# Norm seams of a two-block transformer kernel: order of high and low parts, VectorE's norms and GpSimd's weight pieces

## The chip, the core and the metric

The kernel runs on one core of a Trainium2 chip. The metric is the device time of one execution in microseconds. The engines are TensorE (PE; its weight loads are PEld), VectorE (DVE), ScalarE (ACT), GpSimd (POOL) and SyncE (SP), which issues the weight loads. Each has its own instruction stream, and they meet at semaphores.

## The reference, cut to what matters

Everything is float32: 512 tokens, width 1024. Two blocks of two layers follow each other. The running sum h has a normed copy taken of it before every large product, and the product is added to it:

```
y = h * rsqrt(mean(h*h, axis=-1) + EPS) * gain      # rms norm over the 1024 features
h = h + dsa_attention(norm(h)); h = h + relu(norm(h) @ w_up)**2 @ w_down           # first block, layer 0
k, v, decay = norm(h) @ w_kv; h = h + fox_attention(norm(h), k, v); h = h + mlp(norm(h))
h = norm(h) * g_final
h = h + g1 * gqa_attention(norm(h)*(1+sc1) + sh1); h = h + g2 * mlp(norm(h)*(1+sc2) + sh2)   # second block
h = h + g1 * chunked_gmlp(...); h = h + g2 * mlp(...)
```

In the second block a shift is added behind the norm (sh1, sh2), and the gains, shifts and gates come from a product with ada_w.

## The kernel before, in words

**Data.** h lies transposed in SBUF as HT: eight chunks of 128 features (KC = 8), each 512 tokens wide. The kernel keeps float32 accuracy with three products of numbers of shorter mantissa: an operand x is split in a high part (ScalarE's copy to the type fp32r, in Xhi) and a low part (x less the high part, in Xlo), a weight likewise in whi and wlo. Each product is high times high, high times low and low times high, into one PSUM bank.

**Units of weights.** A GEMM takes its weights in units of 256 columns (1 MB). SyncE loads unit u into raw[u % 2] once the low parts of unit u-2 are out (semaphore lo_done). ScalarE makes whi in two pieces of four chunks (split, L976 to L988, semaphore hi_done), GpSimd makes wlo from them in two pieces (split, L1889 to L1896, lo_done). TensorE waits for each piece ahead of the chunk that needs it (wait_unit_half). A unit has two tiles (j) of 128 output features; each tile is 24 matmuls over the eight chunks, 512 columns wide. The GEMMs "vb" and "gv" have tokens as rows and take a unit as four chunks by 512 columns (tm_wide).

**A seam.** Where a norm stands between two GEMMs and its input is the sum of the first GEMM's outputs, the work is cut in two halves of 256 tokens (h = 0, 1). There are seven, called after the sum (EVENTS): oa, m0, ob, m1, oc, m2 and go, before the normed inputs m0, kv, m1, c, m2, g and m3 (HALVED). m1, oc, m2 and go stand before norms with a shift; m1 has two sums for each chunk, since a final norm and the next block's norm fall together. At a seam:

- TensorE computes the last unit half by half (fm, last). In half 1, after five of the eight chunks of its first tile, come the means of half 0 (norm_means, four matmuls of one column with the mean vector, L450), and after that tile the reciprocal roots are spread to rows by two transposes (norm_rows, L636) into bank 6.
- VectorE (seam, from L1444) adds the last two tiles to HT half by half (add_half, L1407 or L1409), adds their squares to the running sums (add_square_half, L1437), takes reciprocals (recip, L1442), then writes the normed chunk to tmp (L1473, whose second input is the row in PSUM) and the low part Xlo (low, L1460). It takes the norms of chunks one by one and behind each the low part of the chunk two before. A tmp slot of half 0 is used by chunk c and again by chunk c + 4.
- ScalarE (seam, from L1052) squares the last chunks (L1042), takes roots (root, L1048), copies each normed chunk to Xhi (L1068, or L1070 with a shift) and among these makes the two high pieces of the second unit behind the seam.
- GpSimd (seam, from L1911) writes a few of the low parts at the seams oa, m0 and ob (pool_lows: chunks 1 and 3 of half 0 and 3, 5 and 7 of half 1) and, after those of half 0, both low pieces of the second unit. The pieces of the first unit behind the seam were made during the last GEMM's last unit (units).
- TensorE takes the first unit behind the norm half by half (fm with halved, L461 to L492; tm_wide with halved for gv, L583 to L606). For each chunk it waits for the high part and issues four matmuls with it, waits for the low part and issues two with it. Among the chunks of half 0 it puts the means (after chunk 3) and rows (after chunk 5) of half 1. In tm_wide a half has four chunks, and all four banks must be free before it starts; the last one is freed by the last add_half.

For the input g the norms come in the order 0 to 5, 8 to 11, 6, 7, 12 to 15 (fill_order), where 8 to 15 are half 1.

Of the kernel before, what the change touches and what calls it, by code (L numbers as in the profile page):

```python
# [68 lines left out]
SHARED = ("a", "m0", "kv", "qb", "m1")  # L69
# [5 lines left out]
def fill_order(f):  # L75

    if f == "g":
        return [0, 1, 2, 3, 4, 5, 8, 9, 10, 11, 6, 7, 12, 13, 14, 15]
    return list(range(2 * KC if f in HALVED else KC))


def pool_lows(f):

    return () if f not in SHARED else (1, 3, 11, 13, 15) if f in HALVED else (1, 4, 7)

# [50 lines left out]
def body(nc, ctx, t, consts, out):  # L136
# [286 lines left out]
    def tensor_program(pe):  # L423
# [36 lines left out]
        def fm(name, source, chunk, after=None, first=None, halved=None, last=None):  # L460
# [8 lines left out]
            if halved:  # L469
# [3 lines left out]
                for h in range(2):  # L473
                    for c in range(KC):
# [105 lines left out]
        def tm_wide(name, chunk, after=None, halved=None):  # L580
# [5 lines left out]
            if halved:  # L586
# [4 lines left out]
                for h in range(2):  # L591
                    for c in range(KC // 2):
# [3 lines left out]
                        for q in (2 * h, 2 * h + 1):  # L596
                            pe.matmul(bank[(gm.tile + q) % 4][:], Xhi[:, c, q * P:(q + 1) * P], hi[:, c, :], start=(c == 0), stop=False)
                            pe.matmul(bank[(gm.tile + q) % 4][:], Xhi[:, c, q * P:(q + 1) * P], lo[:, c, :], start=False, stop=False)
                        wait_part(halved, KC * h + c)
                        for q in (2 * h, 2 * h + 1):  # L600
                            m = pe.matmul(bank[(gm.tile + q) % 4][:], Xlo[:, c, q * P:(q + 1) * P], hi[:, c, :], start=False, stop=False)
                        if h == 0 and c == 1:
                            norm_means(e, 1, 1)
                        if h == 0 and c == 2:
                            norm_rows(e, 1)
# [362 lines left out]

    def xq_base(f):
# [4 lines left out]
    def scalar_program(act):  # L974
# [77 lines left out]
        def seam(e, name, f, shift, gain=None):  # L1052
# [7 lines left out]
            for p, k in enumerate(fill_order(f)):  # L1060
                h, c = k // KC, k % KC
                act_until.wait_ge(xq_done, xq_base(f) + p + 1)
# [4 lines left out]
                if shift is None:  # L1067
                    act.activation(Xhi[:, c, tokens(h)], tmp[c % 4][:, tokens(h)], ACT_F.Copy).then_inc(x_hi, 1)  # L1068
                else:
                    act.activation(Xhi[:, c, tokens(h)], tmp[c % 4][:, tokens(h)], ACT_F.Identity, bias=shift[:, c:c + 1]).then_inc(x_hi, 1)  # L1070
                if p == 3:
# [279 lines left out]
    def vector_program(dve):  # L1351
# [92 lines left out]
        def seam(e, name, f, gain, shift, gate=None, both=1):  # L1444

            g, n, order = GEMM[name].end - 2, EVENTS.index(e), fill_order(f)
# [6 lines left out]
            def low(k):  # L1453
                if k in pool_lows(f):
                    return
                h, c = k // KC, k % KC
                q, hi, lo = tmp[c % 4][:, tokens(h)], Xhi[:, c, tokens(h)].bitcast(F32), Xlo[:, c, tokens(h)]
                dve_until.wait_ge(x_hi, high_parts(f, k))
                add = 0.0 if shift is None else shift[:, c:c + 1]
                dve.scalar_tensor_tensor(lo, q, add, hi, ALU.add, ALU.subtract).then_inc(x_lo, 1)  # L1460
            for p, k in enumerate(order):
                h, c = k // KC, k % KC
                if h == 0 and c >= KC - 2:
                    dve_until.wait_ge(half_set, 2 * n + c - KC + 3)
                else:
                    dve_until.wait_ge(h_set, h_at[c])
                if c >= 4:
                    by_dve, by_pool = low_parts(f, k - 4)
                    dve_until.wait_ge(x_lo, by_dve)
# [664 lines left out]
```

## Time and profile before

| | us |
|---|---|
| median of 3 runs (lowest, highest) | 2625.74 (2623.57, 2627.0) |
| profiled execution, its own time | 2622.09 |
| its span, first to last instruction | 2620.4 |
| mean granted TensorE clock | 0.998 |
| weights and tables read from HBM | 270.19 MB, 104 GB/s over the span |

The profile is of one execution. The span is the time between its first and last instruction; the execution's own time is 1.7 us longer, and it lies 3.65 us under the median. Times in rows are from the span's start. An engine's busy time counts its instructions' spans, which on TensorE overlap, since matmuls are pipelined: the distance from one start to the next is the better measure there. A bracket behind a row gives the idle time before it and what ended that.

### The profile page before, as it was taken

Reading aid. Unit: us, or ns where it says so; the run is one execution under the profiler, and the core shown is the slowest. Engines: PE = TensorE matmul, PEld = TensorE weight load, DVE = VectorE, ACT = ScalarE, POOL = GpSimd, SP = SyncE. Lnnn points to the kernel's source line nnn. Section 1 sums busy time; section 2 is a strip of 40 time slices with the busy share of each in tenths; the row PEclk is TensorE's granted clock in tenths of the full one; section 3 lists DMA queues with packets and bytes.
Section 4 is the critical chain, followed back from the end, with each engine's and each line's share of the span. In section 5 each row is a group of like instructions: output and inputs, shape, how many; then the busy total and the mean of one; then the engine's idle time right before and its main releaser. Section 6 shows DMA issues by size and latency. Waiting matters only on the chain.

```text
span 2620.4 us, 34369 instructions
## 1 busy us (share of the span) xinstructions
PE 2550.3 (97%) x13922; PEld 2088.1 (80%) x13922; DVE 1341.1 (51%) x2288; ACT 992.9 (38%) x1685; POOL 1248.5 (48%) x624
## 2 busy tenths in 40 slices
PE   8989999999999999999999999999999999999999
PEld 5667888888776888888877888888888888888887
DVE  4873899843036599992786531223435223532121
ACT  4474423223347432232467432232324223432231
POOL 4865444444457454444487444444443444444442
PEclk9999999999999999999999999999999999999999
DMA  4102555532320355542210233323422222233322
GB/s 139 58 32 65 173 194 181 184 115 78 97 81 2 114 192 193 193 161 97 97 65 18 81 97 97 97 97 114 136 81 81 97 97 81 81 97 97 99 98 77
DMA packets 260897, 277.12 MB, mean 106 GB/s; under 512 B 7172, under 2 KB 249476, under 8 KB 260484
## 3 DMA queue, kind: packets, MB, share of 16 engines
q1 hardware_dynamic: 259140, 272.31, 32.1%
q8 instruction: 110, 1.80, 0.3%
q10 hardware_dynamic: 1600, 2.62, 0.3%
q14 instruction: 47, 0.39, 0.0%
HBM read 270.19 MB, written 2.10 MB: 104 GB/s over the span
## 4 chain that ended last, share of the span: by engine, by line
PE 83%; DVE 10%; issue 3%; ACT 3%; POOL 1%; DMA 0%; SPq 0%; ACTq 0%; DVEq 0%
PE bank L529 21%; PE bank L530 21%; PE bank L531 21%; DVE acc L1568 3%; PE bank L622 2%; PE bank L624 2%; PE bank L623 2%; PE bank L708 2%; PE bank L663 2%; DVE tmp L1603 2%; PE bank L691 1%; DVE Hlo L1606 1%; PE bank L484 1%; DVE Xlo L1460 1%; PE bank L936 1%
## 5 line engine op out<-in xcount | busy, mean ns | idle before, releaser
L1896 POOL TENSOR_TENSOR wlo<-raw,whi 128x1024 fp32r<-128x1024 f32 (+1 forms) x408 | 990.2, 2448 | 1213.4 <-ACT whi L988 1213.4
L988 ACT ACTIVATE whi<-raw 128x1024 fp32r<-128x1024 f32 (+1 forms) x408 | 405.6, 1040 | 572.6 <-PE bank L531 495.9
L529 PE MATMUL bank<-Xhi,whi 128*128 128x512 f32 (+1 forms) x1568 | 620.5, 396 | 1.4 <-POOL wlo L1896 1.4
L530 PE MATMUL bank<-Xlo,whi 128*128 128x512 f32 (+1 forms) x1568 | 611.4, 390 | 0.0
L531 PE MATMUL bank<-Xhi,wlo 128*128 128x512 f32 (+1 forms) x1568 | 610.5, 389 | 0.0
L529 PE MATMUL bank<-Hhi,whi 128*128 128x512 f32 x976 | 381.9, 391 | 0.0
L530 PE MATMUL bank<-Hlo,whi 128*128 128x512 f32 x976 | 380.3, 390 | 0.0
L531 PE MATMUL bank<-Hhi,wlo 128*128 128x512 f32 x976 | 379.7, 389 | 0.0
L529 PEld LDWEIGHTS bank<-Xhi,whi 128*128 128x128 f32 (+1 forms) x1568 | 293.3, 187 | 70.1 <-issue 6.6
L531 PEld LDWEIGHTS bank<-Xhi,wlo 128*128 128x128 f32 (+1 forms) x1568 | 293.4, 187 | 63.8
L530 PEld LDWEIGHTS bank<-Xlo,whi 128*128 128x128 f32 (+1 forms) x1568 | 293.4, 187 | 61.4 <-issue 1.7
L1568 DVE SCALAR_TENSOR_TENSOR acc<-ada,cond,acc 128x256 f32<-128x256 f32 x336 | 272.7, 812 | 12.0
L1394 DVE SCALAR_TENSOR_TENSOR HT<-bank,MOD,HT 128x512 f32<-128x512 f32 x90 | 67.3, 751 | 385.3 <-PE bank L531 365.9
L1603 DVE SCALAR_TENSOR_TENSOR tmp<-tmp 128x512 f32<-128x512 f32 x128 | 134.1, 1048 | 229.9 <-ACT tmp L1132 229.9
L1132 ACT ACTIVATE tmp<-bank 128x512 f32<-128x512 f32 x128 | 76.6, 598 | 407.7 <-PE bank L531 400.0
L531 PEld LDWEIGHTS bank<-Hhi,wlo 128*128 128x128 f32 x976 | 183.3, 188 | 38.5
L529 PEld LDWEIGHTS bank<-Hhi,whi 128*128 128x128 f32 x976 | 183.2, 188 | 37.8
L530 PEld LDWEIGHTS bank<-Hlo,whi 128*128 128x128 f32 x976 | 183.3, 188 | 37.5
L1606 DVE SCALAR_TENSOR_TENSOR Hlo<-tmp,Hhi 128x512 fp32r<-128x512 f32 x128 | 116.8, 913 | 13.9 <-ACT Hhi L1136 0.5
L1392 DVE TENSOR_TENSOR HT<-bank,HT 128x512 f32<-128x512 f32 x72 | 49.0, 690 | 142.8 <-PE bank L531 142.8
L622 PE MATMUL bank<-whi,Xhi 128*128 128x512 f32 x240 | 94.6, 394 | 0.0
L623 PE MATMUL bank<-wlo,Xhi 128*128 128x512 f32 x240 | 93.5, 389 | 0.0
(303 smaller groups left out, 3475.5 us busy)
## 6 DMA issues: line engine op xcount, KB each, us to landing
ada<-in_ada_w SPq DMA_DIRECT2D x48, 1024.0 KB, 5.1
raw<-in_w_up SPq DMA_DIRECT2D x32, 1024.0 KB, 5.4
raw<-in_w_down SPq DMA_DIRECT2D x32, 1024.0 KB, 5.0
raw<-in_mlp_w_in SPq DMA_DIRECT2D x32, 1024.0 KB, 5.3
raw<-in_mlp_w_out SPq DMA_DIRECT2D x32, 1024.0 KB, 5.1
raw<-in_gmlp_w_in SPq DMA_DIRECT2D x24, 1024.0 KB, 5.0
raw<-in_gmlp_w_out SPq DMA_DIRECT2D x12, 1024.0 KB, 5.2
raw<-in_w_in_a SPq DMA_DIRECT2D x8, 1024.0 KB, 5.2
```

The lines of the kernel that those rows point to most:

```text
L529: pe.matmul(b[0:rows, :], whi[s][:, c, j:j + rows], hi[:, c, :], start=(c == 0), stop=False)
L530: pe.matmul(b[0:rows, :], whi[s][:, c, j:j + rows], lo[:, c, :], start=False, stop=False)
L531: m = pe.matmul(b[0:rows, :], wlo[s][:, c, j:j + rows], hi[:, c, :], start=False, stop=(c == KC - 1))
L622: pe.matmul(b[:], Xhi[:, c, q * P:(q + 1) * P], hi[:, k, :], start=(c == 0), stop=False)
L623: pe.matmul(b[:], Xhi[:, c, q * P:(q + 1) * P], lo[:, k, :], start=False, stop=False)
L988: act.activation(whi[u % 2][:, c0:c1, 0:k], src[:, c0:c1, 0:k], ACT_F.Copy).then_inc(hi_done, 1)
L1132: act.activation(tmp[v % 2][:], bank[(gm.tile + o) % 4][:], ACT_F.Relu).then_inc(up_q, 1)
L1394: d = dve.scalar_tensor_tensor(HT[:, o, :], b[:], gate[:, o:o + 1], HT[:, o, :], ALU.mult, ALU.add)
L1568: dve.scalar_tensor_tensor(a[:], src[:, c, :], cd[:, c:c + 1], a[:], ALU.mult, ALU.add).then_inc(ada_step, 1)
L1603: dve.scalar_tensor_tensor(r[:], tmp[v % 2][:], 1.0, tmp[v % 2][:], ALU.mult, ALU.mult).then_inc(up_r, 1)
L1606: dve.scalar_tensor_tensor(Hlo[g % 2][:, o, :], r[:], 1.0, Hhi[g % 2][:, o, :].bitcast(F32), ALU.mult, ALU.subtract).then_inc(h_lo, 1)
L1896: pool.tensor_tensor(wlo[u % 2][:, c0:c1, 0:k], src[:, c0:c1, 0:k], whi[u % 2][:, c0:c1, 0:k].bitcast(F32), ALU.subtract).then_inc(lo_done, 1)
```

## The change

Five things are done at the seams.

1. TensorE, first unit behind a norm: for each half all high parts of the chunks are taken first, then all low parts. The means of half 1 stand after chunk 5 (chunk 2 in tm_wide), the rows of half 1 between the high and the low parts of half 0.
2. VectorE: per half eight norms in a row, then eight low parts in a row. The second sum of chunk 6 stands after the fourth norm of half 0, the add of chunk 7 after the eighth, its sum after the second low part, the reciprocal after the sixth. Low parts without a shift are a tensor_tensor instead of a scalar_tensor_tensor with the constant 0. The eight norms have eight slots: chunks 0 to 3 lie in the first halves of the four tmp tiles, 4 to 7 in the second halves.
3. GpSimd makes no low parts of activations at seams any more; VectorE makes all of them.
4. GpSimd's weight pieces get waits. The second piece of the first unit behind the seam waits until both sums of half 0 are done (sum_half). The first piece of the second unit waits for the eighth low part of half 0, its second piece for the last low part of half 1; for g it has no wait of its own.
5. ScalarE: the second unit's first high piece comes after the eight copies of half 0 and ahead of the second root, its second high piece after the last copy of half 1 (after the fourth for g). The order for g is now 0 to 15.

```diff
-SHARED = ("a", "m0", "kv", "qb", "m1")
+SHARED = ("a", "qb")
...
 # TensorE, fm with halved (tm_wide alike, with means after chunk 2)
                             pe.matmul(b[:, tokens(h)], wlo[s][:, c, j * P:(j + 1) * P], hi[:, c, tokens(h)], start=False, stop=False)
+                        if h == 0 and c == 5:
+                            norm_means(e, 1, 1 + (e == "m1"))
+                    if h == 0:
+                        norm_rows(e, 1)
+                    for c in range(KC):
                         wait_part(halved, KC * h + c)
...
-                        if h == 0 and c == 3:
-                            norm_means(e, 1, 1 + (e == "m1"))
-                        if h == 0 and c == 5:
-                            norm_rows(e, 1)
...
 # ScalarE, seam
+            for h in range(2):
...
+                for c in range(KC):
+                    act_until.wait_ge(xq_done, xq_base(f) + KC * h + c + 1)
...
+                    if h and c == (3 if f == "g" else 7):
+                        split(u + 1, (1,))
+                if h == 0:
                     square_half(e, g + 1, KC - 1, 1, gain)
                     split(u + 1, (0,))
-                if p == 5:
                     root(e, 1)
-                if p == 6:
-                    split(u + 1, (1,))
...
 # VectorE, seam (normed(c) is tmp[c % 4][:, tokens(c // 4)])
+            for h in range(2):
+                for c in range(KC):
...
+                    dve.scalar_tensor_tensor(normed(c), HT[:, c, tokens(h)], gain[:, c:c + 1], bank[6 + h][:, tokens(h)], ALU.mult, ALU.mult).then_inc(xq_done, 1)
+                    if h == 0 and c == 3:
+                        add_square_half(e, KC - 2, 1, both)
+                if h == 0:
+                    add_half(e, g + 1, KC - 1, 1, gate)
+                for c in range(KC):
...
+                    if shift is None:
+                        dve.tensor_tensor(lo, normed(c), hi, ALU.subtract).then_inc(x_lo, 1)
+                    else:
+                        dve.scalar_tensor_tensor(lo, normed(c), shift[:, c:c + 1], hi, ALU.add, ALU.subtract).then_inc(x_lo, 1)
+                    if h == 0 and c == 1:
+                        add_square_half(e, KC - 1, 1, both)
+                    if h == 0 and c == 5:
+                        recip(e, 1)
...
 # GpSimd, units (last is the event's name in the last GEMM before a seam)
-                    split(gm.unit + i + 1)
+                    split(gm.unit + i + 1, (0,))
+                    if last and i == len(gm.widths) - 1:
+                        pool_until.wait_ge(sum_half, square_base(last)[2] + 2 * (1 + (last == "m1")))
+                    split(gm.unit + i + 1, (1,))
...
 # GpSimd, seam
+            u = GEMM[name].unit + len(GEMM[name].widths) + 1
+            pool_until.wait_ge(x_lo, low_parts(f, KC - 1)[0])
+            split(u, (0,))
+            if f != "g":
+                pool_until.wait_ge(x_lo, low_parts(f, 2 * KC - 1)[0])
+            split(u, (1,))
```

## Rows read from the trace of the kernel before

**Rows 1.** The page, part 1: busy us (share of the span) and instructions.

```profile
PE 2550.3 (97%) x13922; PEld 2088.1 (80%) x13922; DVE 1341.1 (51%) x2288; ACT 992.9 (38%) x1685; POOL 1248.5 (48%) x624
```

**Rows 2.** Waits of TensorE: who for whom, us in total, times, longest.

```profile
PE bank L484 <- DVE Xlo L1460: 16.6, 15, 1.9
...
PE bank L450 <- DVE rstd L1437: 5.5, 6, 1.3
...
PE bank L450 <- DVE gained L1437: 2.4, 1, 2.4
...
PE bank L601 <- DVE Xlo L1460: 1.1, 2, 0.9
```

**Rows 3.** Timelines of VectorE and TensorE, seam m2: start, us, instruction, idle before.

```profile
1830.09 0.48 DVE L1409 SCALAR_TENSOR_TENSOR HT<-bank,MOD,HT 128x256 f32<-128x256 f32 x1
...
1830.93 0.47 PE L597 MATMUL bank<-whi,Xhi 128*128 128x512 f32 x1 [1.06 <-DVE HT L1409]
```

**Rows 4.** Timeline of TensorE, seam oa.

```profile
257.32 0.28 PE L550 MATMUL bank<-Xhi,wlo 128*128 128x256 f32 x1
258.81 0.60 PE L450 MATMUL bank<-mean,rstd 128*128 128x1 f32 x4 [1.21 <-DVE rstd L1437]
...
263.54 0.28 PE L480 MATMUL bank<-Xhi,whi 128*128 128x256 f32 x1
...
264.25 0.28 PE L480 MATMUL bank<-Xhi,whi 128*128 128x256 f32 x1
...
270.00 0.29 PE L481 MATMUL bank<-Xhi,wlo 128*128 128x256 f32 x1
272.00 0.50 PE L484 MATMUL bank<-Xlo,whi 128*128 128x256 f32 x2 [1.71 <-DVE Xlo L1460]
```

**Rows 5.** Timeline of VectorE, seam oa.

```profile
255.19 2.33 DVE L1437 SCALAR_TENSOR_TENSOR rstd<-rstd,held 128x256 f32<-128x256 f32 x1 [1.74 <-ACT held L1042]
...
260.97 0.47 DVE L1473 SCALAR_TENSOR_TENSOR tmp<-HT,V,bank 128x256 f32<-128x256 f32 x1
...
263.74 0.42 DVE L1407 TENSOR_TENSOR HT<-bank,HT 128x256 f32<-128x256 f32 x1 [0.26 <-PE bank L550]
...
267.34 0.48 DVE L1473 SCALAR_TENSOR_TENSOR tmp<-HT,V,bank 128x256 f32<-128x256 f32 x1
...
270.23 1.71 DVE L1460 SCALAR_TENSOR_TENSOR Xlo<-tmp,Xhi 128x256 fp32r<-128x256 f32 x1
```

**Rows 6.** Timeline of GpSimd, seam oa.

```profile
252.47 4.77 POOL L1896 TENSOR_TENSOR wlo<-raw,whi 128x1024 fp32r<-128x1024 f32 x2 [6.12 <-ACT whi L988]
...
265.64 2.37 POOL L1896 TENSOR_TENSOR wlo<-raw,whi 128x1024 fp32r<-128x1024 f32 x1 [0.89 <-ACT whi L988]
269.30 2.36 POOL L1896 TENSOR_TENSOR wlo<-raw,whi 128x1024 fp32r<-128x1024 f32 x1 [1.29 <-ACT whi L988]
```

**Rows 7.** Windows at m1: stretch, length, busy by engine, granted clock, DMA share, GB/s.

```profile
1252.00:1254.00 2.00, 1.96 (x14) 1.96 (x15) 0.17 (x1) 0.41 (x2) 0.00 (x0) 0.85 0.00 0
1254.00:1256.00 2.00, 2.00 (x11) 2.00 (x11) 1.04 (x3) 0.66 (x2) 0.00 (x0) 0.50 0.00 0
1256.00:1258.00 2.00, 2.00 (x16) 2.00 (x16) 2.00 (x6) 1.47 (x4) 0.00 (x0) 0.80 0.00 0
```

**Rows 8.** Timelines of VectorE and TensorE, seam m1.

```profile
1247.73 2.61 DVE L1437 SCALAR_TENSOR_TENSOR gained<-gained,held 128x256 f32<-128x256 f32 x1
...
1252.04 0.61 PE L450 MATMUL bank<-mean,rstd 128*128 128x1 f32 x4 [2.41 <-DVE gained L1437]
```

**Rows 9.** Timelines of VectorE and ScalarE: norms (oa), low parts (oc), a high piece.

```profile
261.88 0.87 DVE L1473 SCALAR_TENSOR_TENSOR tmp<-HT,V,bank 128x256 f32<-128x256 f32 x2
...
1488.32 1.26 DVE L1460 SCALAR_TENSOR_TENSOR Xlo<-tmp,MOD,Xhi 128x256 fp32r<-128x256 f32 x3
...
264.52 1.05 ACT L988 ACTIVATE whi<-raw 128x1024 fp32r<-128x1024 f32 x1
```

**Rows 10.** The page, part 6: DMA issues, KB each, median us to landing.

```profile
raw<-in_w_up SPq DMA_DIRECT2D x32, 1024.0 KB, 5.4
```

More of the change, by code:

```diff
@@ L75, in fill_order @@
 def fill_order(f):
-    if f == "g":
-        return [0, 1, 2, 3, 4, 5, 8, 9, 10, 11, 6, 7, 12, 13, 14, 15]
     return list(range(2 * KC if f in HALVED else KC))
 def pool_lows(f):
-    return () if f not in SHARED else (1, 3, 11, 13, 15) if f in HALVED else (1, 4, 7)
+    return (1, 4, 7) if f in SHARED else ()
 def high_parts(f, k):
@@ L598, in tm_wide @@
                             pe.matmul(bank[(gm.tile + q) % 4][:], Xhi[:, c, q * P:(q + 1) * P], lo[:, c, :], start=False, stop=False)
+                        if h == 0 and c == 2:
+                            norm_means(e, 1, 1)
+                    if h == 0:
+                        norm_rows(e, 1)
+                    for c in range(KC // 2):
                         wait_part(halved, KC * h + c)
@@ L601, in tm_wide @@
                             m = pe.matmul(bank[(gm.tile + q) % 4][:], Xlo[:, c, q * P:(q + 1) * P], hi[:, c, :], start=False, stop=False)
[L602 to L605, printed above, removed]
                 m.then_inc(half_done, 1)
@@ L967, in tensor_program, with normed @@
                 m.then_inc(o_full, 1)
+    def normed(c):
+        return tmp[c % 4][:, tokens(c // 4)]
     def xq_base(f):
@@ L1059, in seam @@
             square_half(e, g, KC - 2, 1, gain)
-            for p, k in enumerate(fill_order(f)):
-                h, c = k // KC, k % KC
-                act_until.wait_ge(xq_done, xq_base(f) + p + 1)
+            for h in range(2):
                 if h:
@@ L1444, in seam @@
         def seam(e, name, f, gain, shift, gate=None, both=1):
-            g, n, order = GEMM[name].end - 2, EVENTS.index(e), fill_order(f)
+            g, n = GEMM[name].end - 2, EVENTS.index(e)
             for c in (KC - 2, KC - 1):
@@ L1451, in seam @@
             add_half(e, g, KC - 2, 1, gate)
[L1453 to L1460, printed above, removed]
@@ L1485, in seam @@
                     dve_until.wait_ge(z_root, 2)
                     dve.reciprocal(zcol[:, NT:2 * NT], zcol[:, 0:NT]).then_inc(z_recip, 1)
-            low(order[-2])
-            low(order[-1])
         def rotation_sin(r, rope, rows=P):
@@ L1888, in gpsimd_program, with split @@
         pool_until = Until(pool)
-        def split(u):
+        def split(u, parts=range(2)):
             src, k = raw[u % 2], unit_width(u)
-            for n in range(2):
+            for n in parts:
                 c0, c1 = 4 * n, 4 * n + 4
@@ L1896, in split, with units @@
                 pool.tensor_tensor(wlo[u % 2][:, c0:c1, 0:k], src[:, c0:c1, 0:k], whi[u % 2][:, c0:c1, 0:k].bitcast(F32), ALU.subtract).then_inc(lo_done, 1)
-        def units(name, each=None, ahead=0):
+        def units(name, each=None, ahead=0, last=None):
             gm, o = GEMM[name], 0
@@ L1913, in seam @@
         def seam(name, f):
-            for h in range(2):
-                for k in pool_lows(f):
-                    if k // KC == h:
-                        c = k % KC
-                        pool_until.wait_ge(x_hi, high_parts(f, k))
-                        pool.tensor_tensor(Xlo[:, c, tokens(h)], tmp[c % 4][:, tokens(h)], Xhi[:, c, tokens(h)].bitcast(F32), ALU.subtract).then_inc(x_lop, 1)
-                if h == 0:
-                    split(GEMM[name].unit + len(GEMM[name].widths) + 1)
+            u = GEMM[name].unit + len(GEMM[name].widths) + 1
[4 more added lines that the diff above has]
+            split(u, (1,))
         def rotation(r, rope, rows=P):
@@ L1969, in gpsimd_program @@
         attend("a")
-        units("oa")
+        units("oa", last="oa")
         seam("oa", "m0")
@@ L1974, in mlp @@
             for f, g in MLP_ORDER:
-                units(f"m{m}{f}{g}", ahead=int((f, g) == ("u", 0)))
+                units(f"m{m}{f}{g}", ahead=int((f, g) == ("u", 0)), last=f"m{m}" if (f, g) == ("d", 3) and m < 3 else None)
         mlp(0)
@@ L1983, in gpsimd_program @@
         attend("b")
-        units("ob")
+        units("ob", last="ob")
         seam("ob", "m1")
@@ L1997, in gpsimd_program @@
         attend("c")
-        units("oc")
+        units("oc", last="oc")
         seam("oc", "m2")
@@ L2004, in gpsimd_program @@
             units(f"gu{g}")
-            units(f"go{g}")
+            units(f"go{g}", last="go" if g == 2 else None)
         seam("go2", "m3")
```

43 lines of the change are left out of this document (15 added, 28 removed).

## The prediction

> **What bounds the kernel now.** I read the page's busy line first: TensorE is busy 97% of the span, and every other engine has about half the span or more free [rows 1]. So a change pays only where it takes time out of TensorE's row. The waits of TensorE name the places: 16.6 us in 15 waits for the low parts that VectorE writes (L1460), 5.5 and 2.4 us in 7 waits for the sums of squares (L1437), 1.1 us in 2 waits for low parts in the wide GEMM [rows 2], and 1.1 in one ahead of it [rows 3]. All 25 lie at the seven seams (a seam: the norm between two GEMMs, on tokens in two halves). The waits inside attention stay as they are.
>
> At the first seam the timeline shows the shape. Matmuls of 256 columns start every 0.12 us; the one at 257.32 is followed by the means at 258.81, and between 270.00 and 272.00 nothing starts [rows 4]. A row's "idle" is smaller than the time lost: 258.81 - 257.32 - 0.12 = 1.37 us against 1.21 shown, since a matmul's 0.28 us overlaps the next start. I add 0.16 to each wait.
>
> VectorE shows why. A sum that takes 0.42 us takes 2.33 at 255.19, and a low part 1.71 at 270.23; both end within 0.3 us of the end of a GpSimd weight piece (252.47 to 257.24, 269.30 to 271.66) [rows 5, 6]. Under the piece from 265.64 to 268.01 a norm, one of whose inputs is in PSUM, takes 0.48 at 267.34, against 0.47 elsewhere [rows 5, 6]. So what is locked is the VectorE operation with two SBUF inputs beside a GpSimd piece of 2.4 us, and norms are not.
>
> The bill before: 16.6 + 5.5 + 2.4 + 1.1 + 1.1 = 26.7 us, plus 25 x 0.16 = 4.0, plus three gaps of 0.2 to 0.3 too short to be listed (0.6 together). At seam m1 the granted clock is 0.85, 0.50 and 0.80 in three stretches of 2 us, behind a wait of 2.41 us [rows 7, 8]: its lower level, 1.2 GHz, for part of each. That costs 2 x (0.15 + 0.50 + 0.20) = 1.7 us of work at full clock. In all 33.0 us.
>
> **The first sums.** The second piece of the first unit behind the seam now waits until both half-0 sums are done. At the first seam the sum at 255.19 then ends at 255.6. TensorE puts 15 matmuls of half 1 before the means, so half 0 ends 15 x 0.12 before 257.44, near 255.7, and the second add runs 255.85 to 256.27, ScalarE squares in as long, by 256.7, and the sum ends at 257.2, before TensorE asks at 257.44: 1.37 us saved, once each at oa, ob, oc and go, and the 0.4 us at m0 and m2. At m1 there are two sums for each chunk and the first piece is not gated: it still holds the first sum until 1247.73. The second took 2.61 us and ended at 1250.34, and the means came 1.70 later [rows 8]; at 0.43 it ends at 1248.16, the means come at 1249.86, and TensorE arrives at 1252.04 - 2.41 - 0.16 = 1249.47: 2.57 us lost become 0.4. With so small a gap I take the clock to stay up (1.7 us; at worst nothing of it).
> The released piece runs from 257.2 to 259.6, as the norms begin, and its weights are wanted four chunks into the unit, at about 264.2: nothing.
>
> **The first unit, half 0.** T is its start: 263.54 before, 262.17 after. VectorE now does eight norms in a row, the pace being 0.39 (0.87 for two) [rows 9]. The first starts at 259.6 (260.97 before, less 1.37), a sum stands after the fourth, and the eighth ends at T+1.0 (-2.57 + 8 x 0.39 + 0.34 + 0.08); the add of the last chunk ends at T+1.4, its square on ScalarE at T+2.0. Two lows, then the sum, end at T+2.6 with a shift and T+2.4 without (three shifted lows take 1.26, 0.40 apart; an operation of 0.42 that overlaps the next by 0.08, as norms do, comes every 0.34) [rows 5, 9]. TensorE does a chunk's six matmuls in 0.71, so the four high ones in 0.48 [rows 4], and asks for the sum after six chunks, T+2.88: in time. ScalarE now has a weight piece of 1.05 us ahead of the second root [rows 9]; it ends at T+2.9 to T+3.1, before the means do (T+3.4). A root of 0.3, then the reciprocal behind the sixth low: T+4.0 to T+4.25. TensorE asks for it after eight chunks and the means (0.44), T+4.3. That fits with 0.05 to 0.3 us to spare. The last high part of the half is read at T+3.8 and there at T+1.6. At m1 the doubled sum ends at T+3.2: 0.4 us of wait.
>
> **Half 1.** Lows of half 0 take 0.24 a chunk on TensorE [rows 4], so half 1 starts at T+6.4. The transposed row is there at T+4.7, norm 8 and its copy make T+5.7 to T+6.1. Norms come at 0.39 against 0.48 of the matmuls. Lows 8 to 15 run from about T+8 and end at T+10.6, or T+11.3 with a shift; TensorE reads its last low at about T+12.0. The gated piece of the second unit starts at T+4.8 to T+5.2, when half 0's lows are out, and covers norms only, which it does not lock. So the lows' waits (the longest at oa 272.00 - 270.00 - 0.12 = 1.88) go to zero.
> VectorE takes over five lows a seam from GpSimd at oa, m0, ob (3 x 5 x 0.34 = 5.1 us) and that is inside the times above. Tensor_tensor for the no-shift lows costs the same: an add of that kind and shape is 0.42 [rows 5]; bounds -0.1 to +0.1 each, nothing on TensorE.
>
> **The second unit.** Its second piece starts when all sixteen lows are out and ends 2.5 us later, T+13.1 (T+13.8 with a shift, T+14.6 at m1). TensorE leaves the first unit at T+12.2 and reaches the fifth chunk 12 matmuls of twice the width later, 12 x 0.24 = 2.9 at most, about T+15.0 [rows 4]: 0.4 to 1.9 us to spare. The load of the raw slot waits in SP's queue for that piece, with the load of ada_w, tri and tsum behind it: issued about 275.3 instead of 271.7 [rows 6]. It lands 5.4 us later, 280.7 [rows 10]; ScalarE wants it when the second unit's 48 matmuls are through, T+12.2 + 10.9 = 285.3, so 4.6 us of cover are left.
>
> **Seam m2 (GEMM gv).** The wide unit writes four banks, so it waits for the last add of half 1. Before, the add ended at 1830.57 and TensorE began at 1830.93, having lost 1.22 [rows 3]. It could now go at 1829.71 - 0.36 = 1829.35, which is T here. The add comes after eight norms and ends at T+1.4, the first matmul follows at T+1.8: 1.8 us lost. Here alone the second piece is not gated by the last lows but follows ScalarE's copy 11. Half 0's highs, means and rows (4 x 0.91 + 0.7) bring norm 8 to 1835.8, so the norms end at 1839.0, copy 11 at 1838.0 and ScalarE's piece at 1839.1. GpSimd's piece and low 8 start together, and the next low waits to 1841.8, on TensorE about 0.9 us, against 1.42 before (the 1.1 of its two waits [rows 2], plus 0.16 each). Saved in all with the first sum's 0.4: 0.3.
> The Trainium skill (SBUF — State Buffer, "Who interferes with whom") has it that whichever of the two engines starts first keeps the shared pair for its whole instruction, and the other blocks fully. The trace agrees in the one direction with the 1.71 us low [rows 5]. By that rule the order at 1839 decides: nothing lost if VectorE's eight lows kept GpSimd out throughout, 1.3 if GpSimd came first.
>
> **The sum.** 33.0 before. Left after: m1 0.8 (0.4 + 0.4), m2 2.7, oc and go 0.1 together, 3.6. Gain 29.4. I take 28: each remaining sync costs a few hundredths more than its row says and three of the fits above are within 0.2 us. The profiled run took 2622.09 us (span 2620.4), which becomes 2594. It stands 3.65 under the median of the runs, 2625.74, from which 28 leaves **2598**.
>
> **Rivals.**
> (a) The second row comes late. The weight piece ahead of the root, or the six lows ahead of the reciprocal, take 1 to 1.5 us more than I count and TensorE waits at the rows, at six seams: 28 - 7.5 = 20.5, 2605. For: the margin is 0.05 to 0.3 us. Against: ScalarE's piece is through 0.3 us before the means are.
> (b) The lock only moves: the gated pieces meet the sum after the fourth norm or the lows of half 1 at most seams, at up to 2 us each: 14 us given back, 2612. Against: pieces are timed by VectorE's own semaphores, except at m2.
> (c) Nothing: the change keeps GpSimd out of the sums but TensorE then waits for something else as long, a copy or a bank: 2623 to 2628. Only m2 shows such a bank.
> (d) Slower: the second unit's weights come late. The place is the fifth chunk of that unit, the price its lateness, seam by seam. It decides from 0.4 us late at m1 and 1.9 at oa on; to be slower by 5.3 us in all it must cost (28 + 5.3) / 7 = 4.8 us a seam, so lows 8 to 15 would have to end near T+17 rather than T+11, at over 1.0 us each. Time 2632. For: it is the one wait added to a weight path. Against: lows that no GpSimd piece overlaps take 0.42 to 0.48.
>
> **Chances.** Forecast 0.63 (2594 to 2602), (a) 0.18, (b) 0.07, (c) 0.04, (d) 0.04; 0.04 for more gain than counted (2592: clock and all waits gone). A difference under 0.2%, 5.3 us, can't be told from none here. Faster 0.92, same 0.04, slower 0.04. Range 2591 to 2610: it holds the forecast, (a), and all but the far part of (b).
>
> **What would show it.** Right: TensorE's waits for L1437 and L1460 (24.5 us) fall below 3; no VectorE sum or low at a seam over 0.6 us except the first sum at m1 and one low at m2; the clock at m1 stays near 1.0; norms stand eight in a row at 0.39. Wrong: waits for the reciprocal at the rows (a), GpSimd pieces over sums (b), TensorE waiting for wlo in a second unit (d), or the gap before gv above 2.5 us.

## The result, and the profile after

| | before | changed |
|---|---|---|
| median of 4 runs (lowest, highest), us | 2625.59 (2623.57, 2627.0) | 2587.03 (2586.45, 2588.09) |
| profiled execution, own time / span | 2622.09 / 2620.4 | 2586.45 / 2585.1 |
| ratio of the times, 95% interval | | 0.9854 [0.9837, 0.9871] |

The change saves 38.6 us where I forecast 28, and 2587.03 lies under my range of 2591 to 2610. Run again beside ten runs of the kernel before it saved 35.0 (2588.23 against 2623.26, ratio 0.9862 [0.9847, 0.9877]). The direction and the places were right; the size was not. Ratios compare fast executions alone, so an execution of 12637.5 us, one of seven of the kernel with the sum's gate alone, counts for none.

The busy line of the page answers to [rows 1]: TensorE has lost 10.8 us of busy time and the span 35.3, so most of the gain is time in which TensorE stood.

```profile
PE 2539.5 (98%) x13922; PEld 2083.2 (81%) x13922; DVE 1330.0 (51%) x2303; ACT 988.4 (38%) x1685; POOL 1237.2 (48%) x609
```

The waits of TensorE answer to [rows 2]. The 25.6 us for L1437 and L1460 (24.5, and 1.1 in the wide GEMM) have become 0.6 (L1440 is the sum now, L1474 and L1476 the lows). At the seams only these three are left in the list. The first of them, ahead of gv, names a copy of ScalarE, but it ends with the bank's last add, as shown further down:

```profile
PE bank L596 <- ACT Xhi L1074: 1.7, 1, 1.7
...
PE bank L605 <- DVE Xlo L1476: 0.4, 1, 0.4
...
PE bank L448 <- DVE gained L1440: 0.2, 1, 0.2
```

VectorE at the first seam, against [rows 5]: the sum at 254.45 takes 0.43 where its counterpart at 255.19 took 2.33, norms stand eight in a row (3.22) and so do the lows of half 1 (2.77, where one alone took 1.71).

```profile
254.45 0.43 DVE L1440 SCALAR_TENSOR_TENSOR rstd<-rstd,held 128x256 f32<-128x256 f32 x1 [1.74 <-ACT held L1046]
...
256.01 0.43 DVE L1440 SCALAR_TENSOR_TENSOR rstd<-rstd,held 128x256 f32<-128x256 f32 x1 [0.48 <-ACT held L1046]
...
262.22 0.41 DVE L1410 TENSOR_TENSOR HT<-bank,HT 128x256 f32<-128x256 f32 x1
262.56 0.75 DVE L1474 TENSOR_TENSOR Xlo<-tmp,Xhi 128x256 fp32r<-128x256 f32 x2
263.22 0.42 DVE L1440 SCALAR_TENSOR_TENSOR rstd<-rstd,held 128x256 f32<-128x256 f32 x1
...
265.04 0.17 DVE L1445 RECIPROCAL rcol<-rcol 128x2 f32<-128x2 f32 x1
...
266.08 3.22 DVE L1465 SCALAR_TENSOR_TENSOR tmp<-HT,V,bank 128x256 f32<-128x256 f32 x8 [0.23 <-PE bank L636]
269.22 2.77 DVE L1474 TENSOR_TENSOR Xlo<-tmp,Xhi 128x256 fp32r<-128x256 f32 x8
```

GpSimd there, against [rows 6]: one piece released by the sum, one by the eighth low, one by the sixteenth, and none of them beside a sum or a low part.

```profile
256.51 2.38 POOL L1891 TENSOR_TENSOR wlo<-raw,whi 128x1024 fp32r<-128x1024 f32 x1 [2.38 <-DVE rstd L1440]
265.94 2.42 POOL L1891 TENSOR_TENSOR wlo<-raw,whi 128x1024 fp32r<-128x1024 f32 x1 [7.04 <-DVE Xlo L1474]
272.07 2.40 POOL L1891 TENSOR_TENSOR wlo<-raw,whi 128x1024 fp32r<-128x1024 f32 x1 [3.71 <-DVE Xlo L1474]
```

TensorE, against [rows 4] and [rows 8]: at the first seam the means follow 0.12 us behind the matmul before them, with no wait; at m1 (the last row) 0.22 is left of 2.41.

```profile
256.58 0.28 PE L549 MATMUL bank<-Xhi,wlo 128*128 128x256 f32 x1
256.70 0.50 PE L448 MATMUL bank<-mean,rstd 128*128 128x1 f32 x4
...
1234.57 0.61 PE L448 MATMUL bank<-mean,rstd 128*128 128x1 f32 x4 [0.22 <-DVE gained L1440]
```

And the windows of m1, against [rows 7]: the granted clock (the number behind the five engines) is 1.00 where it had been 0.85, 0.50 and 0.80.

```profile
1234.00:1236.00 2.00, 1.78 (x15) 1.58 (x15) 0.56 (x3) 0.40 (x3) 1.41 (x1) 1.00 0.00 0
1236.00:1238.00 2.00, 2.00 (x19) 2.00 (x18) 1.28 (x5) 0.78 (x3) 0.96 (x1) 1.00 0.00 0
1238.00:1240.00 2.00, 2.00 (x19) 2.00 (x19) 2.00 (x7) 1.79 (x6) 0.00 (x0) 1.00 0.00 0
```

**The measure for all that follows.** Both kernels issue the same 13922 matmuls, so I counted them from the first and took, at each seam, the time from the start of one well before it to the start of one well behind it. Seven such stretches and the rest of the kernel make up the distance from the first matmul to the last. Against the kernel before, in us:

```
                    oa     m0     ob     m1     oc     m2     go    sum   rest
forecast         -4.64  -3.63  -5.02  -6.67  -4.57  -0.3   -4.55  -29.4
changed          -5.07  -4.03  -5.45  -7.34  -5.51  -0.91  -5.51  -33.8   -1.4
run again        -5.07  -4.03  -5.45  -7.32  -5.51  -0.95  -5.51  -33.8   +1.2
```

(The forecast row shares my 29.4 out over the seams by the waits and short gaps of before at each.) The seams repeat within 0.04 us. The rest differs by 2.6 between two executions of one program. So the change is worth 33.8 us at the seams, and the 35.0 of the long comparison is near it. The other 4.8 us of the first 38.6 lie outside the seams, where the profiles show no steady gain: -1.4 and +1.2 us here, and +0.9 and +0.2 in the two runs below whose seams are the same. I take the 4.8 for scatter.

### The profile page after: what moved, and what is told of

It reads as the page before. It is cut to its first block, busy times and chain, and to the rows that moved or that the text cites. A ratio compares the mean times of both kernels' runs of the same rounds, so it can differ in the third digit from the quotient of the medians.

```text
span 2585.1 us, 34367 instructions
## 1 busy us (share of the span) xinstructions
PE 2539.5 (98%) x13922; PEld 2083.2 (81%) x13922; DVE 1330.0 (51%) x2303; ACT 988.4 (38%) x1685; POOL 1237.2 (48%) x609
## 4 chain that ended last, share of the span: by engine, by line
PE 87%; DVE 8%; ACT 2%; issue 2%; POOL 1%; DMA 0%; SPq 0%; ACTq 0%; DVEq 0%
PE bank L528 22%; PE bank L529 21%; PE bank L530 21%; DVE acc L1563 2%; PE bank L622 2%; PE bank L623 2%; PE bank L624 2%; PE bank L663 2%; PE bank L708 2%; DVE tmp L1598 2%; PE bank L691 1%; DVE Hlo L1601 1%; PE bank L547 1%; PE bank L487 1%; PE bank L936 1%
## 5 line engine op out<-in xcount | busy, mean ns | idle before, releaser
L624 PE MATMUL bank<-whi,Xlo 128*128 128x512 f32 x240 | 93.5, 390 | 0.0
```

Of the source, the lines that this page charges most:

```text
L624: m = pe.matmul(b[:], Xlo[:, c, q * P:(q + 1) * P], hi[:, k, :], start=False, stop=(c == KC - 1))
```

## Experiments

Unless said otherwise an edit is made in the changed kernel. "Seams" is the sum of the seven stretches against the kernel before, and its cost that against the run again.

**The change once more.** 

> The changed kernel as it is, beside the kernel before in the same rounds. Its profile before this run moved by 35.3 us of span, the medians by 38.6. Theory A (the seams are the whole gain; the other 3 us are scatter of the executions of before): the difference of the medians is 34 to 37 us. Rival B (the change takes 3 us more in unprofiled executions, for instance at the start): again 38 to 39 us.

Measured 2588.23, ratio 0.9862 [0.9847, 0.9877], shown above.

**The sum's gate alone, in the kernel before.**

```diff
-                    split(gm.unit + i + 1)
+                    split(gm.unit + i + 1, (0,))
+                    if last and i == len(gm.widths) - 1:
+                        pool_until.wait_ge(sum_half, square_base(last)[2] + 2 * (1 + (last == "m1")))
+                    split(gm.unit + i + 1, (1,))
```

> The kernel before with one part of the change: the second low piece of the first unit waits for the half-0 sums. Theory A (the piece locks VectorE's sum, and a wait costs TensorE its idle time plus 0.26): the steps seen at the first sums come, 1.5 at oa, ob, oc, go, 0.5 at m0 and m2, 3.6 at m1: 10.7 us faster, 2615. Rival C (lock only moves to the sum or lows behind): under 4 us. My terms on record would make it 1.37 x 4 + 0.8 + 2.2 + 1.7 = 10.2.

Measured 2614.77 against 2623.26, ratio 0.997 [0.9958, 0.9982]; seams -9.3. Of the waits for the sums 0.2 us is left, at m1, and the 15 for lows are still there, 1.1 us shorter in all:

```profile
PE bank L484 <- DVE Xlo L1460: 15.5, 15, 1.9
```

The clock took part of the gain back. It was down for some 3 us at m1 as in the kernel before, now behind a wait for a low part, and for as long at m0, where it had been up, so that m0 came out 0.56 us longer than before instead of 0.5 shorter:

```profile
634.00:636.00 2.00, 2.00 (x11) 2.00 (x11) 2.00 (x6) 1.05 (x3) 0.73 (x1) 0.50 0.90 274
```

**The change without that gate.**

```diff
-                    split(gm.unit + i + 1, (0,))
-                    if last and i == len(gm.widths) - 1:
-                        pool_until.wait_ge(sum_half, ...)
-                    split(gm.unit + i + 1, (1,))
+                    split(gm.unit + i + 1)
```

> The changed kernel without that same wait. Theory A: 10.7 us slower than the changed kernel, the waits for L1437's counterpart (the sums) back at 5.5 + 2.4 us idle, clock at m1 down again for some 3 us. Rival D (the new order alone gives the sums room): within 3 us of the changed kernel.

Measured 2602.27, ratio 0.9917 [0.9902, 0.9932]: 14.0 over the changed kernel, 13.4 at the seams. The waits come back to the tenth as in [rows 2]:

```profile
PE bank L448 <- DVE rstd L1440: 5.5, 6, 1.3
...
PE bank L448 <- DVE gained L1440: 2.4, 1, 2.4
```

By the terms of the prediction this gate was worth 4 x 1.37 + 2 x 0.4 + 2.2 + 1.7 = 10.2. Two things make up the difference. First the price of a wait. At the five seams where the clock stayed up in this run (oa, m0, ob, oc, m2) the stretches grew by 1.48 + 0.43 + 1.49 + 1.61 + 0.46 = 5.47 us for five waits of 4.2 us listed idle (5.5 less go's 1.3), so each wait costs 0.25 more than its row says, not 0.16. Second the clock. At m1 and at go it stood at its lower level (a granted clock of 0.50) behind the wait, at m1 for about 7 us, twice as long as before:

```profile
1242.00:1244.00 2.00, 0.88 (x5) 0.88 (x5) 0.83 (x2) 0.61 (x2) 0.00 (x0) 0.78 0.00 0
1244.00:1246.00 2.00, 2.00 (x10) 2.00 (x11) 0.17 (x1) 0.41 (x2) 0.00 (x0) 0.50 0.00 0
...
1248.00:1250.00 2.00, 2.00 (x11) 2.00 (x11) 2.00 (x7) 2.00 (x6) 0.00 (x0) 0.51 0.00 0
```

**No waits for lows.**

```diff
-            pool_until.wait_ge(x_lo, low_parts(f, KC - 1)[0])
-            split(u, (0,))
-            if f != "g":
-                pool_until.wait_ge(x_lo, low_parts(f, 2 * KC - 1)[0])
-            split(u, (1,))
+            split(u)
```

> The changed kernel without the waits of the second unit's low pieces for VectorE's low parts; each piece follows ScalarE's high piece. Theory A: the first piece starts at T+3 and locks lows 3 to 7 and with them the second reciprocal, TensorE waits about 1.8 at the rows; the second starts at T+9.6 and locks lows of half 1, another 1.2; with 0.26 for each wait 3.3 us a seam, 21 us in all at seven seams (at gv the second piece has no such wait, so 2 there). Rival E (eight norms in a row already put the pieces under operations that aren't locked): under 5 us.

Measured 2598.83, ratio 0.9904 [0.9889, 0.9918]: 10.6 more, 11.4 at the seams (about 1.1 each at oa, m0 and ob, 1.7 at oc and go, 4.4 at m1, 0.3 at m2). I had expected 21. VectorE and GpSimd at the first seam say why it is half of that:

```profile
263.98 1.43 DVE L1474 TENSOR_TENSOR Xlo<-tmp,Xhi 128x256 fp32r<-128x256 f32 x4
265.46 0.17 DVE L1445 RECIPROCAL rcol<-rcol 128x2 f32<-128x2 f32 x1
265.54 2.74 DVE L1474 TENSOR_TENSOR Xlo<-tmp,Xhi 128x256 fp32r<-128x256 f32 x2
...
271.34 2.76 DVE L1474 TENSOR_TENSOR Xlo<-tmp,Xhi 128x256 fp32r<-128x256 f32 x8
```

```profile
264.54 3.12 POOL L1891 TENSOR_TENSOR wlo<-raw,whi 128x1024 fp32r<-128x1024 f32 x1 [5.22 <-ACT whi L992]
272.89 3.47 POOL L1891 TENSOR_TENSOR wlo<-raw,whi 128x1024 fp32r<-128x1024 f32 x1 [5.23 <-ACT whi L992]
```

The piece of 264.54 is released 0.56 us into four lows. They run on undisturbed (1.43 for four; 1.42 in the changed kernel); it is the piece that takes 3.12 instead of 2.4. Only at the reciprocal, which opens a gap in VectorE's row of such operations, does it get in, and then two lows take 2.74 instead of 0.74. The second piece falls 1.55 us into eight lows and waits them all out, 3.47 long, at no cost to VectorE.

So it went at five seams. At m1 and m2 the first piece, released 0.59 and 0.47 us into the four lows, did get in among them, and they took 3.78 and 3.80 us, against 1.66 in the changed kernel:

```profile
1246.51 3.78 DVE L1476 SCALAR_TENSOR_TENSOR Xlo<-tmp,MOD,Xhi 128x256 fp32r<-128x256 f32 x4
```

At m1 the clock also stood at its lower level for about 7 us (0.50 from 1250 to 1256), which is part of the 4.4; no run takes the two apart.

**The second of these waits alone taken out.**

```diff
-            if f != "g":
-                pool_until.wait_ge(x_lo, low_parts(f, 2 * KC - 1)[0])
```

> The changed kernel without the wait of the second unit's second low piece for the last low part of half 1; the first piece still waits. Theory J, from the kernel without both waits (a GpSimd piece issued at 272.89 beside eight lows that took 2.76 us lasted 3.47): VectorE keeps the port while its two-input operations follow each other without a gap, and the piece waits. Then this wait is worth nothing: every seam as in the changed kernel within 0.1 us, and all 11.4 us of both waits belong to the first. Rival K (who starts first holds, and a waiting piece comes in between two lows): 1.2 to 1.5 us more at six seams.

One run, 2588.13; every seam within 0.02 of the run again. VectorE, then GpSimd:

```profile
270.06 2.76 DVE L1474 TENSOR_TENSOR Xlo<-tmp,Xhi 128x256 fp32r<-128x256 f32 x8
```

```profile
266.77 2.42 POOL L1891 TENSOR_TENSOR wlo<-raw,whi 128x1024 fp32r<-128x1024 f32 x1 [7.04 <-DVE Xlo L1474]
271.61 3.46 POOL L1891 TENSOR_TENSOR wlo<-raw,whi 128x1024 fp32r<-128x1024 f32 x1 [2.43 <-ACT whi L992]
```

At all six seams where this wait had stood the piece came 1.55 to 1.72 us into the eight lows and stayed out. The second wait is worth nothing; the first is worth all 11.4, what it saves of the clock at m1 included.

**Smaller pieces instead of waits.** Four instructions of 128x256 instead of one of 128x1024, and no wait for lows.

```diff
-            pool_until.wait_ge(x_lo, low_parts(f, KC - 1)[0])
-            split(u, (0,))
-            if f != "g":
-                pool_until.wait_ge(x_lo, low_parts(f, 2 * KC - 1)[0])
-            split(u, (1,))
+            split(u, size=1)
```

> The changed kernel without the waits of the second unit's low pieces for VectorE, and with these two pieces cut in four instructions each, 0.6 us long. Theory H (whichever engine starts holds the port for one instruction): VectorE's operation is held for at most 0.6 us and the two take turns, so lows come every 1.0 us rather than 0.34 while a piece runs: 1.0 to 2.0 us a seam lost, 7 to 14 us slower than the changed kernel, and faster than the kernel with whole pieces and no waits. Rival I (GpSimd keeps the port through all four): the same as with whole pieces, about 21 us slower.

Measured 2591.29, ratio 0.9875 [0.986, 0.9889]; cost 3.75 at the seams, none at oa, m0 and ob, 1.3 to 1.5 at m1, oc and go, and m2 0.5 shorter. I had expected 7 to 14. Two lows now take 1.62 (263.05) where the whole piece made them 2.74. It gets two thirds of what the first wait brings.

**TensorE's order of before.** Lows directly behind each chunk's highs, means and rows where they were.

```diff
-                        if h == 0 and c == 5:
-                            norm_means(e, 1, 1 + (e == "m1"))
-                    if h == 0:
-                        norm_rows(e, 1)
-                    for c in range(KC):
                         wait_part(halved, KC * h + c)
...
+                        if h == 0 and c == 3:
+                            norm_means(e, 1, 1 + (e == "m1"))
+                        if h == 0 and c == 5:
+                            norm_rows(e, 1)
```

> The changed kernel with TensorE's order of before: high and low parts of a chunk one behind the other, means of half 1 after chunk 3 and rows after chunk 5 (1 and 2 in the wide unit). VectorE, ScalarE and GpSimd as changed. Theory A: TensorE reaches low 0 at T+0.5 and it is there at T+1.8 (1.3 lost), low 8 at T+8.2 and it is there at T+10.1 (1.9 lost), and 0.26 for each: 3.7 us at six seams, none at gv, 22 us slower than the changed kernel. Rival F (TensorE's order is neutral, the gain is in GpSimd's waits): within 3 us.

Measured 2614.86 against 2625.79, ratio 0.9965 [0.9952, 0.9978]; cost 28.9 at the seams. Every seam waits twice for lows, gv too (L599), where I had expected no wait:

```profile
PE bank L482 <- DVE Xlo L1474: 9.5, 6, 1.9
PE bank L482 <- DVE Xlo L1472: 8.6, 6, 1.8
...
PE bank L599 <- DVE Xlo L1474: 2.3, 2, 1.4
```

Not all of the 28.9 is waiting. Behind such a wait the clock stood at its lower level for some 3 us at oa, m0, m1 and go, where it had been up in the changed kernel. Matmuls of 256 columns then start every 0.21 us instead of 0.12, about 1.5 us lost each time (an estimate from the 16 or so such starts). The window at oa:

```profile
274.00:276.00 2.00, 2.00 (x10) 2.00 (x11) 2.00 (x7) 0.99 (x2) 0.00 (x0) 0.53 0.00 0
```

These stretches, some 6 us together, and the 2.2 at gv more than cover the 7 us by which the cost exceeds the 22 expected.

**Norms and lows in turn on VectorE,** a norm, then the low part two chunks back. It is not quite VectorE's order of before: the last add and its sum stand here behind the eighth norm and the reciprocal behind the last low, where the kernel before had them behind the fourth, fifth and sixth norm.

```diff
                     dve.scalar_tensor_tensor(normed(c), ...)
-                    if h == 0 and c == 3:
+                    if c >= 2:
+                        low(h, c - 2)
+                    if h == 0 and c == 0:
                         add_square_half(e, KC - 2, 1, both)
+                    if h == 0 and c == 7:
+                        add_half(e, g + 1, KC - 1, 1, gate)
+                        add_square_half(e, KC - 1, 1, both)
+                low(h, 6)
+                low(h, 7)
                 if h == 0:
...
+                    recip(e, 1)
```

> The changed kernel with VectorE's norms and low parts in turn, the low part two chunks behind the norm, the last add and its sum after the eighth norm and the reciprocal after the last low of half 0; TensorE's order and GpSimd's waits as changed. Theory A: the sum comes 1.4 us late, and in half 1 high parts come every 0.73 us (0.79 with a shift) against 0.48 that TensorE takes, 1.3 to 2 us late at the last; with 0.26 a wait 3.2 us a seam, 20 us slower than the changed kernel. Rival L (the row of eight norms matters only for where the pieces fall): under 5 us.

Measured 2613.73, ratio 0.9957 [0.9942, 0.9972]; cost 24.8 at the seams. The second half's sum is late, since the add of chunk 7 stands behind six lows, and so is the bank of gv:

```profile
PE bank L448 <- DVE rstd L1440: 8.2, 5, 1.9
...
PE bank L596 <- DVE HT L1412: 4.2, 1, 4.2
```

Here too the clock is in the cost: it was at its lower level for some 3 us at ob, m1 and oc and for about 7 at m2 and go, as in this window at go:

```profile
2256.00:2258.00 2.00, 2.00 (x11) 2.00 (x11) 0.51 (x2) 0.00 (x0) 1.22 (x1) 0.50 0.00 0
```

In these two runs either order alone keeps 5 to 9 of the 33.8 us, about what the sum's gate brings by itself. That VectorE's rows bring little without TensorE's order is shown. The reverse is shown only for a late add and a late reciprocal: in this run their places and the taking in turn were changed together, and a run with the add kept early is missing.

**The low parts' instruction.**

```diff
-                        dve.tensor_tensor(lo, normed(c), hi, ALU.subtract).then_inc(x_lo, 1)
+                        dve.scalar_tensor_tensor(lo, normed(c), 0.0, hi, ALU.add, ALU.subtract).then_inc(x_lo, 1)
```

> The changed kernel with scalar_tensor_tensor and the constant 0 for the low parts without a shift, as before. Every theory that I hold: the same time within 1 us, since both forms last 0.42 us. If tensor_tensor is the cheaper form, the lows at oa, m0 and ob take longer in the profile and the row of half 1 comes later.

Measured 2588.13, ratio 0.9862 [0.9847, 0.9877]; every seam within 0.02. No difference.

**The kernel before without the shift.**

```diff
-                add = 0.0 if shift is None else shift[:, c:c + 1]
+                add = 0.0
```

> The kernel before, leaving the shift out of the low parts at the four seams that have one (c, m2, g, m3), so that a low part takes 0.42 instead of 0.48 and a norm with its low 0.73 instead of 0.79 a chunk. It tests a term that the working on record lacks: oc and go gave 5.5 us where the waits and their restarts explain 5.0. Theory M (in half 1 TensorE, at 0.72 a chunk, is paced by VectorE at 0.79): oc and go 0.4 to 0.6 us shorter than in the kernel before, m1 about as much, oa, m0 and ob equal within 0.05. Rival N (the rest lies elsewhere, in the matmuls' own starts): no seam moves by over 0.1.

One run, 2621.83. Stretches against the kernel before: oa, m0 and ob 0.0, m1 -0.51, oc -0.66, m2 -0.33; go +0.80, where this run had a stretch of lower clock. At seam oc a norm and a low came every 0.79 us in the kernel before and every 0.73 here:

```profile
1484.77 0.47 DVE L1473 SCALAR_TENSOR_TENSOR tmp<-HT,GM,bank 128x256 f32<-128x256 f32 x1
1485.16 0.47 DVE L1460 SCALAR_TENSOR_TENSOR Xlo<-tmp,MOD,Xhi 128x256 fp32r<-128x256 f32 x1
1485.56 0.47 DVE L1473 SCALAR_TENSOR_TENSOR tmp<-HT,GM,bank 128x256 f32<-128x256 f32 x1
```

```profile
1484.34 0.47 DVE L1473 SCALAR_TENSOR_TENSOR tmp<-HT,GM,bank 128x256 f32<-128x256 f32 x1
1484.73 0.41 DVE L1460 SCALAR_TENSOR_TENSOR Xlo<-tmp,Xhi 128x256 fp32r<-128x256 f32 x1
1485.07 0.47 DVE L1473 SCALAR_TENSOR_TENSOR tmp<-HT,GM,bank 128x256 f32<-128x256 f32 x1
```

TensorE does a chunk in 0.71. So behind a shift it was held to VectorE's pace, 0.08 us a chunk, in gaps too short for any list of waits.

**Two tries at a better version.** For gv: the last add after the sixth norm, and the second piece behind four lows of half 1. With it, in the first of the two, a gate on m1's first piece.

```diff
-                if h == 0:
-                    add_half(e, g + 1, KC - 1, 1, gate)
+                    if h == 0 and c == (5 if f == "g" else 7):
+                        add_half(e, g + 1, KC - 1, 1, gate)
...
+                    if last == "m1" and i == len(gm.widths) - 1:
+                        pool_until.wait_ge(sum_half, square_base(last)[2] + 4)
...
-            if f != "g":
-                pool_until.wait_ge(x_lo, low_parts(f, 2 * KC - 1)[0])
+            pool_until.wait_ge(x_lo, low_parts(f, (KC + 3) if f == "g" else 2 * KC - 1)[0])
```

> The changed kernel with three edits at the places where TensorE still waits: at gv the last add stands after the sixth norm rather than the eighth, and the second unit's second low piece waits for the fourth low part of half 1; at m1 the first low piece of the first unit waits for the sums too. Theory A (TensorE's idle there plus 0.26 a wait): the wait ahead of gv falls from 1.7 to 0.9, the one for the low parts (0.4) and the one for the sums at m1 (0.2) go: 1.3 idle and two waits, 2 us faster than the changed kernel. Rival G (the pieces come late to the second unit instead): a wait for wlo at gv, no gain.

Measured 2586.77, ratio 0.986 [0.9843, 0.9876]: m2 1.00 better, m1 0.26 worse, since TensorE's wait for the sums there grew from 0.2 to 0.6 instead of going. Without the gate at m1:

> The changed kernel with the two edits at gv alone (last add after the sixth norm, second low piece waits for the fourth low of half 1). In the run with three edits the seam m2 was 1.0 us shorter and m1 0.26 longer. Theory A: m2 1.0 shorter, all other seams equal within 0.05; the median about 1 us under the changed kernel's, too little to tell in the medians.

Measured 2587.56, ratio 0.9858 [0.9842, 0.9875]: m2 0.97 better, the other seams as they were. With the add 0.8 us earlier TensorE's wait ahead of gv fell from 1.7 to 0.9, and the low's wait of 0.4 went: the first wait was for the bank. By the seams this is the fastest version (34.8 against 33.8); the medians (2587.56 against 2588.23) can't tell it from the changed kernel.

## Why the prediction was too small

**The mechanism held.** Counted from T, the unit's first matmul (261.32 now), the forecasts at the first seam were: first norm T-2.57, second sum done T+2.4, means T+2.88, reciprocal T+4.0 to T+4.25, rows T+4.3, half 1 T+6.4, last low T+10.6, second piece done T+13.1. Measured: -2.56, +2.32, +2.88, +3.89, +4.28, +6.42, +10.67, +13.15. No rival came: TensorE waits for no reciprocal (a), the bank is missed only at m2 (c), and no second unit waits for weights anew (d). Of (b) there is a little more than I foresaw. I named the first sum at m1 and one low at m2 as the only ones over 0.6 us. The first unit's first piece, which has no gate, is also over the first sum at m0 and at m2 (1.29 and 1.28 us), at no cost to TensorE:

```profile
612.05 1.29 DVE L1440 SCALAR_TENSOR_TENSOR rstd<-rstd,held 128x256 f32<-128x256 f32 x1 [0.49 <-ACT held L1046]
```

**The step that failed is the sizing of the bill before, 33.0 us, and the discount behind it.** Between the 28 forecast and the 38.6 measured lie 10.6 us: 1.4 of discount, 4.4 at the seams, and 4.8 outside them, which no term of the sum covers. At the seams 33.8 came against 29.4:
- **The price of a wait.** "I add 0.16 to each wait." The run without the sum's gate has it at 0.25. Of 25 waits 3 are left: 22 x 0.09 = 2.0 us. The 0.16 was worked out to the start of the first matmul behind the wait; but the next ones start late too. The means after a wait take 0.61 for four, without one 0.50 (rows above), and before gv the first matmul is 0.31 ahead of the second, the following ones 0.23:

```profile
1802.22 0.47 PE L596 MATMUL bank<-whi,Xhi 128*128 128x512 f32 x1 [1.68 <-ACT Xhi L1074]
1802.53 0.39 PE L597 MATMUL bank<-wlo,Xhi 128*128 128x512 f32 x1
1802.76 0.40 PE L596 MATMUL bank<-whi,Xhi 128*128 128x512 f32 x1
```

- **The unlisted gaps behind a shift.** I had 0.6 for "three gaps", single ones ahead of a low at m1, oc and go. The pace is another term: with TensorE held to 0.79 a chunk, each chunk's first matmul of lows starts 0.08 late in half 1. The run without the shift gave 0.5 to 0.7 back at m1 and oc; at go, where that run had the lower clock, I take 0.5 by the same row. About 1.5 us more.
- **m1 and m2.** At m1 the waits for the two pairs of sums cost 0.38 and 0.29 from start to start, instead of 0.4 and 0.4. At m2 the forecast was 0.3 and 0.9 was measured. The wait for the bank was as forecast (1.68 idle for "1.8 us lost"; the add of the last chunk ends at 1801.83, TensorE starts at 1802.22), but the low's was 0.36 idle, 0.5 from start to start, not 0.9, though the lock itself came as drawn: the eight lows take 5.39 there instead of 3.25.

```profile
1801.35 0.48 DVE L1412 SCALAR_TENSOR_TENSOR HT<-bank,MOD,HT 128x256 f32<-128x256 f32 x1
...
1810.08 5.39 DVE L1476 SCALAR_TENSOR_TENSOR Xlo<-tmp,MOD,Xhi 128x256 fp32r<-128x256 f32 x8
```

At m2 0.2 of the 0.6 is the price of its waits, counted above already. So these make 2.0 + 1.5 + 0.1 + 0.4 = 4.0 of the difference of 4.4. The discount from 29.4 to 28 stood for late syncs after the change; none came, as the margins of 0.05 to 0.3 us were real. And the lower end of my range, 2591, allowed a gain of 34.7: the 33.8 of the seams alone would lie inside, the 4.8 outside them took it over the edge. I had left nothing for the scatter of medians: those of the kernel before in four comparisons were 2625.59, 2623.26, 2625.79 and 2624.65.

**The parts.** The sum's gate was sized at 10.2; it measured 9.3 alone and 13.4 inside the change. The clock lies between the two: alone it left the stretch at m1 and one came at m0, and inside the change, leaving the gate out brought about 7 us of lower clock at m1 and 3 at go. The orders of TensorE and VectorE were tested only as said above, and neither kept more than 9 us alone. The first wait for lows is worth 11.4 and the second, which I took to be as necessary, nothing. These parts overlap and do not add up to 33.8. Tensor_tensor for the no-shift lows is nothing, as forecast.

**The rule on the shared port.** I quoted the Trainium skill (SBUF — State Buffer, "Who interferes with whom"): who starts first keeps the pair for its whole instruction. The 1.71 us low agrees. The second pieces at six seams in the runs without their wait go beyond it: each was released under one low of 0.42 to 0.48 us and was kept out by the lows behind it as well, for 1.1 to 1.4 us (3.47 and 3.80 long instead of 2.4). Other pieces got in between two lows, at m1 and m2. So the rule by single instructions, which I had drawn on for m2, does not by itself tell who is next.

## What to carry to other kernels

When TensorE is the bound and an engine beside it is locked out by another's long instruction, pay for order, not for speed: put the operations that can be locked back to back, and release the other engine's long instruction by a semaphore when that row is through. Where it comes late into the row anyway, leave the semaphore out: the second wait brought nothing here. Price a TensorE wait at its listed idle plus about 0.25 us, and compare the pace of producer and consumer per chunk as well, since gaps under the list's threshold add up. Change a consumer's order (all highs, then all lows) and the producer's together: here neither brought much alone.

## What was not expected of the hardware

- **A row of VectorE operations kept GpSimd out.** Of the pieces released while lows followed back to back, all 12 that came 1.55 to 1.72 us into a row of eight stayed out to its end, in the two runs without the second wait. Released earlier in a row it went both ways. At 0.47 us into four lows a piece got in at m2 and stayed out at oc and go, in one run. At m2 a piece that started 0.11 us into the eight lows got in behind the first of them in the changed kernel (the 5.39 above), and in the run without waits for lows, at the same 0.11, it waited all of them out (3.25 for the eight):

```profile
1821.39 3.25 DVE L1476 SCALAR_TENSOR_TENSOR Xlo<-tmp,MOD,Xhi 128x256 fp32r<-128x256 f32 x8
```

What decides it is open; no run here tells.
- **The lower clock comes and goes between executions of one program.** In the two profiled executions of the changed kernel no seam had it, but the first had a single stretch of some 3 us at the lower level inside attention and the other three (at the start and twice in attention; one of them in the windows below). That is most likely the 2.6 us by which their rests differ; no run takes it apart. The stretches at seams in the experiments above stand in one profile each, so how much of those costs another execution would show is open.

```profile
828.00:830.00 2.00, 1.02 (x22) 0.74 (x18) 1.19 (x6) 1.34 (x5) 1.59 (x2) 0.99 0.00 0
830.00:832.00 2.00, 2.00 (x20) 1.67 (x20) 0.00 (x0) 0.66 (x2) 2.00 (x2) 0.50 0.00 0
```
